# Fewer, longer visits: two transposes of a residual tile and two gating mixtures taken together on TensorE

## The reference

```
h = x @ w_in + b_in          # q, k, v, z_a, u_g, v_g, z_g, g_a, g_g
y_a = sliding_window_attention(q, k, v, sinks) * silu(z_a)
vn  = layer_norm(gelu(v_g))                      # 4 chunks of 128 tokens, 4 groups of 128 columns
mixed = einsum('gts,bcsgd->bctgd', causal(w_s), vn) + b_s
y_g = gelu(u_g) * mixed * silu(z_g)
merged = sigmoid(g_a) * (y_a @ w_branch_attn) + sigmoid(g_g) * (y_g @ w_branch_gmlp)
x = layer_norm(ALPHA * x + merged @ w_out + b_out)
```

## Time and profile before

| | |
|---|---|
| median of 3 runs | 1525.86 us |
| profiled execution | 1526.24 us, span 1524.3 us |
| PE, DVE, ACT, POOL busy | 99%, 71%, 38%, 25% of the span |
| mean granted TensorE clock | 0.999 |
| `bra` 0, first layer | starts at 1067.37 us |
| `bra` 2, first layer | starts at 1072.90 us |
| evacuation of `bra` 0, first layer | 1071.61 to 1072.29 us |

### The profile page before, as it was taken

One profiled execution on the slowest core, in us unless ns is written; L12 is line 12 of the kernel. 1 busy time (PEld: TensorE's weight loads), 2 busy tenths in 40 slices (PEclk: granted clock), 3 DMA queues, 4 the chain that ended last, 5 costly groups with the idle time before them and its releaser, 6 DMA issues.

```text
span 1524.3 us, 29860 instructions
## 1 busy us (share of the span) xinstructions
PE 1514.7 (99%) x12255; PEld 1357.0 (89%) x12255; DVE 1082.2 (71%) x1844; ACT 574.2 (38%) x1022; POOL 375.0 (25%) x334
## 2 busy tenths in 40 slices
PE   9999999999999999999999999999999999999998
PEld 9999999999998989988998898888888988888886
DVE  6656565766879877886998678779616787787246
ACT  5323222253435434442544455472112245541121
POOL 0000000022423404231342024334530044343510
PEclk9999999999999999999999999999999999999999
DMA  5322332232434544344355243554324325552331
GB/s 173 111 84 83 95 100 84 89 106 90 136 110 123 149 126 121 116 132 134 102 146 161 72 137 97 171 155 136 105 83 145 124 84 152 151 169 87 127 117 55
DMA packets 168021, 180.60 MB, mean 118 GB/s; under 512 B 16620, under 2 KB 137872, under 8 KB 167888
## 3 DMA queue, kind: packets, MB, share of 16 engines
q1 hardware_dynamic: 129584, 141.99, 30.7%
q10 hardware_dynamic: 38224, 36.52, 7.8%
q0 software_dynamic: 80, 0.20, 0.1%
HBM read 156.67 MB, written 22.02 MB: 117 GB/s over the span
## 4 chain that ended last, share of the span: by engine, by line
PE 96%; DVE 1%; DMA 1%; ACT 1%; ACTq 0%; issue 0%; SPq 0%; DVEq 0%
PE acc L431 28%; PE acc L433 28%; PE acc L432 28%; PE aux L597 1%; PE aux L431 1%; PE aux L433 1%; PE aux L432 1%; PE aux L657 1%; PE aux L659 1%; PE aux L649 1%; PE aux L1450 1%; DMA pt_second<-p_turn 1%; PE aux L578 1%; PE aux L1493 0%; PE aux L589 0%; PE aux L1416 0%
## 5 line engine op out<-in xcount | busy, mean ns | idle before, releaser
L431 PE MATMUL acc<-xhis,whi 128*128 128x264 f32 (+2 forms) x1848 | 608.1, 329 | 0.0
L433 PE MATMUL acc<-xhis,wlo 128*128 128x264 f32 (+2 forms) x1848 | 602.0, 326 | 0.2 <-issue 0.2
L432 PE MATMUL acc<-xlos,whi 128*128 128x264 f32 (+2 forms) x1848 | 601.8, 326 | 0.4 <-issue 0.3
L433 PEld LDWEIGHTS acc<-xhis,wlo 128*128 128x128 f32 x1848 | 347.9, 188 | 30.3 <-issue 1.1
L431 PEld LDWEIGHTS acc<-xhis,whi 128*128 128x128 f32 x1848 | 348.0, 188 | 29.1 <-issue 0.3
L432 PEld LDWEIGHTS acc<-xlos,whi 128*128 128x128 f32 x1848 | 348.2, 188 | 27.1
L426 POOL TENSOR_TENSOR wlo<-raw,whi 128x1024 fp32r<-128x1024 f32 x84 | 208.5, 2484 | 364.7 <-DVE whi L2700 364.7
L422 ACT ACTIVATE whi<-raw 128x1024 fp32r<-128x1024 f32 x158 | 164.3, 1048 | 134.5 <-PE acc L433 120.9
L426 DVE TENSOR_TENSOR wlo<-raw,whi 128x1024 fp32r<-128x1024 f32 x81 | 99.8, 1236 | 36.9 <-ACT whi L422 36.7
L2374 DVE TENSOR_TENSOR wlo<-raw,whi 128x1024 fp32r<-128x1024 f32 x77 | 96.1, 1249 | 30.6 <-ACT whi L422 30.5
L2700 DVE CAST whi<-raw 128x1024 fp32r<-128x1024 f32 x84 | 61.2, 733 | 54.0 <-PE acc L433 53.8
(11 more groups left out here) (398 smaller groups left out, 2827.7 us busy)
## 6 DMA issues: line engine op xcount, KB each, us to landing
raw<-in_w_in SPq DMA_DIRECT2D x38, 1024.0 KB, 5.4
raw<-in_hgrn_w_in SPq DMA_DIRECT2D x32, 1024.0 KB, 5.9
raw<-in_pool_w_in SPq DMA_DIRECT2D x15, 1024.0 KB, 5.6
raw<-in_pool_w_out SPq DMA_DIRECT2D x8, 1024.0 KB, 5.0
raw<-in_hgrn_w_out SPq DMA_DIRECT2D x8, 1024.0 KB, 5.1
raw<-in_w_out SPq DMA_DIRECT2D x8, 1024.0 KB, 5.0
v_turn<-vb ACTq DMA_DIRECT2D x8, 544.0 KB, 2.7
raw<-in_pool_w_grp SPq DMA_DIRECT2D x4, 1024.0 KB, 5.1
```

Source lines behind the costliest of these rows:

```text
L431: pe.matmul(dst, stat[0], mov[0], start=first, stop=False)
L432: pe.matmul(dst, stat[0], mov[1], start=False, stop=False)
L433: return pe.matmul(dst, stat[1], mov[0], start=False, stop=last)
```

## The change

Three edits. In the tail, `g2_part(c, 0)` turns all eight blocks of tile `c`, four into each bank, and `g2_part(c, 1)` turns none. In a layer of the second block, the mixtures of groups 0 and 1 are both made after `gg` 1, and those of groups 2 and 3 after `gg` 3; the groups alternate between the two banks of `aux`, so that a group waits only for DVE's bias addition of the group two before it, and the first waits for the last scores of attention to be read from `aux`. DVE and ACT follow, since they read the same order.

```diff
@@ c_slots
-                    if stage in ("gg",) and index < 4:
-                        side.append(("mix", index))
+                    if stage == "gg" and index in (1, 3):
+                        side += [("mix", index - 1), ("mix", index)]
@@ g2_part
                 if j == 0:
                     pe.wait_ge(acc_done[c % 2], (U7 + 8) // 2 + (1 if c < 2 else 0))
-                for n in range(4):
-                    pe.matmul(dst[:, P * n:P * n + P], h[:, 4 * j + n, META + P * c:META + P * c + P],
-                              ident[:, :], start=(n == 0), stop=False, is_transpose=True)
+                    for n in range(KT):
+                        pe.matmul(acc[c % 2][:, n // 4, P * (n % 4):P * (n % 4) + P],
+                                  h[:, n, META + P * c:META + P * c + P],
+                                  ident[:, :], start=(n % 4 == 0), stop=False, is_transpose=True)
@@ side_tensor
                     pe.wait_ge(vn_step, 4 * i + 4)
-                    pe.wait_ge(yg_step, 1 + 12 * i + max(3 * n - 2, 0))
+                    if n == 0:
+                        pe.wait_ge(asc_ready, 1 + 2 * (16 * i + 16))
+                    pe.wait_ge(yg_step, 1 + 12 * i + max(3 * n - 5, 0))
                     for c in range(CH):
-                        mm = pe.matmul(aux[:, 1, P * c:P * c + P], vn[:, c, P * n:P * n + P], wst[:, n, :],
+                        mm = pe.matmul(aux[:, n % 2, P * c:P * c + P], vn[:, c, P * n:P * n + P], wst[:, n, :],
@@ mix_vector
-                                  aux[:, 1, :].rearrange("p (c t) -> p c t", c=CH),
+                                  aux[:, g % 2, :].rearrange("p (c t) -> p c t", c=CH),
```

## The result

| | |
|---|---|
| changed kernel | 1532.05 us, median of 6 runs (1529.32 to 1533.34) |
| kernel before, beside it | 1525.91 us, median of 6 runs (1525.31 to 1526.54) |
| ratio | 1.0037, 95% interval 1.0027 to 1.0047, so +4.1 to +7.2 us |
| profiled execution | 1531.44 us, span 1529.6 us (before 1524.3) |

A forecast was written before the change was run, and what follows sets the result against it. TensorE (PE), busy 99% of the span, was taken as the bound. Two layers' stalls, +4.5 us, less 0.1 for boundaries gave +4.4 on 1525.86, so 1530.3 us; range 1527.0 to 1533.0, the forecast's own 1529.7 to 1531.0.

The forecast's parts named there:

- Boundaries (-0.1 us): Tail and two layers: merging visits saves eight boundaries between products and a visit, 0.013 us each, 0.1 us in all.
- The chain on VectorE (steps 1 to 6): Each layer, groups 0 and 1 to `bra` 2: later VectorE work delays `bra` 0's evacuation, costing TensorE 2.24 us.
- TensorE's restart: At `bra` 2: TensorE starts the waiting multiplication 0.15 us after VectorE's evacuation ends.
- 2.24 us a layer: `bra` 2 starts at 1075.11 instead of 1072.87; over two layers 4.5 us lost.
- floor of 0.2 us a layer: Lower bound at `bra` 2: if GpSimd did not hold VectorE up, the chain is 2.04 us shorter.
- step 2: VectorE, group 1's mixture follows group 0's at once; rounding for `bra` 2 and 3 starts at 1064.04 instead of 1061.51.
- the clock falls in the stall: Rival, chance 0.03: TensorE's clock drops to 1.2 GHz at `bra` 2's stall, 1.7 us more per layer, 1533.7 us.
- The other order at the port: Rival, chance 0.13: GpSimd's second subtraction goes before group 2's first multiplication; 2.97 us a layer, 1531.7 us.
- slack: First layer, `bra` 0's evacuation to `bra` 2's start: 0.46 us to spare after TensorE's 0.15 us restart.

The follow-up runs named there:

- The tail alone: Kernel before with only the tail edit (eight transposes in one visit per tile), mixtures as before: 1525.75 us against 1526.50, ratio 0.9997.
- The held rounding: Changed kernel with VectorE's rounding of the piece for `brg` 0 and 1 moved behind `bra` 0's evacuation: 1526.64 us against the kernel before's 1526.10, ratio 1.0003.
- the two half changes: Changed kernel with only groups 0 and 1 sharing a visit, 1530.31 us; with only groups 2 and 3 sharing, 1526.49; kernel before 1526.50.
- the first pair alone: Changed kernel, but only groups 0 and 1 share a visit, groups 2 and 3 apart: 1530.31 us against the kernel before's 1526.50, ratio 1.0027.
- unfilled stall: Without the nine idle multiplications that another version of the changed kernel ran before `bra` 2's wait; that filled version measured 1530.16 and 1530.42 us.

## Why the prediction was right, and where its size fell short

**Boundaries (-0.1 us).** The visit of eight transposes cost 0.89 us, as predicted. The tail alone made no difference that can be measured, so the 0.1 us itself is not shown.

**The chain on VectorE (steps 1 to 6).** Right, step by step. From the start of the common visit, the end of group 2's second multiplication was put at 5.28 us and came at 5.31; the start of the evacuation at 8.63, and came at 8.67. One detail was off without effect: the first multiplication was not held at all (0.69), since it got in at 1068.21, just ahead of GpSimd's second subtraction (from 1068.28), and the second took the whole hold. TensorE's restart was put at 0.15 us and took 0.06, but its first product then costs 0.11 more. That the two differences nearly cancel is luck. The sum of 2.24 us a layer was 2.28.

**What the loss hangs on.** The prediction put it on GpSimd's second subtraction, with a floor of 0.2 us a layer without it. The held rounding shows just that: 0.2 us. It named the seven operations between visit and evacuation as the mechanism's place; the two half changes show that the first pair, not the second, makes the loss. That is step 2, where VectorE rounds at 1064 instead of 1061.5. With the first pair alone that lateness makes a stall of nearly the same length, 2.1 us, though groups 2 and 3 then meet one subtraction each, as before the change. So the second subtraction is one way to lose this time, and lateness alone is another, which the prediction did not separate.

**The profiled execution.** Its span is 5.3 us longer. 2 x 2.28 less 0.1 is 4.5. The other 0.8 us arise at the opening, which the change does not touch: the same 16 multiplications ran longer. The granted clock reads 1.00 there in both profiles, so these rows do not say why. PE's timeline after and then before:

```profile
3.72 3.48 PE L1169 MATMUL aux<-ones_d 128*128 128x128 f32 x16
...
10.42 0.37 PE L1215 MATMUL acc<-xhis,whi 128*128 128x264 f32 x1
```

```profile
3.71 2.70 PE L1169 MATMUL aux<-ones_d 128*128 128x128 f32 x16
...
9.70 0.37 PE L1215 MATMUL acc<-xhis,whi 128*128 128x264 f32 x1
```

**The median.** 1532.05 lies 1.75 us above the forecast, near the price of one fall of the clock. This is the term that was mis-sized: the rival "the clock falls in the stall" had a chance of 0.03, since the only idleness in the trace before that lowered the clock was the 3.4 us at its end. I took the shorter stall to be harmless. In three of the five profiles with an unfilled stall the clock fell behind it (two of the changed kernel's four, and that with groups 0 and 1 together), and by the mean clock in about half of the runs. What it costs was nearly right, 1.6 us against 1.7; but it came once, in the first layer, in each of the three profiles, and never in the second. That the median lies inside the stated range is in part luck: the range was drawn past the other order at the port, which did not come, and the case of the clock, at 1533.7, lay outside it.

**The other order at the port** did not occur in any of the four profiles of the changed kernel, though the margin was 0.07 to 0.09 us.

## What to carry to other kernels

When one engine is never idle, a batch of side work is paid for by the queue it delays: follow the in-order engine that takes the results to the first operation that the bound engine waits for, and see what slack that has now (0.46 us by the prediction, 0.55 with the restart of 0.06 us that was measured). An operation that is moved may also come to lie beside another engine's burst, and then it takes that burst's time and not its own. Price a stall of TensorE twice, once as the wait and once, with a chance, as products at half the clock behind it.

## What was not expected of the hardware

- Behind a gap of 2.4 us between the starts of two products (2.2 with groups 0 and 1 together) TensorE's clock went to its 1.2 GHz level in three profiles of five. TensorE's other waits in these traces, up to 1.6 us at the opening and 0.7 us for attention's transfers, were not followed by a fall. Why it happens in one execution and not in another, the runs do not settle. Nor is it known what made the slower runs of the kernel before: its one profile shows a low clock only at the end, and so do those of the other versions without a stall.
- Two subtractions in a row on GpSimd do not shut VectorE out for both: in the gap between them a multiplication went through in 0.69 us, and only the next one was held; it took 2.77.
- The boundary between the one-pass products and the float32 passes of a transpose or a mixture costs TensorE 0.01 us by the estimate from the earlier trace rows, little enough that merging eight of them cannot be measured.
